# A two-layer hybrid trunk on one core: the last down projection with tokens on partitions, its norm by token blocks, and the token half moved outside the three products

## What is computed

```python
def rms_norm(x, w):
    y = x * lax.rsqrt(jnp.mean(x * x, axis=-1, keepdims=True) + NORM_EPS)
    return y * w

def swiglu(x, w_gate, w_up, w_down):
    return (jax.nn.silu(x @ w_gate) * (x @ w_up)) @ w_down
...
    for layer in range(DEPTH):          # 2
        nw = norm_w[layer]
        f = swiglu(rms_norm(h, nw[0]), ffn_w_gate[layer, 0], ffn_w_up[layer, 0], ffn_w_down[layer, 0])
        h = h + 0.5 * rms_norm(f, nw[1])
        ...                             # token mixer, residual
        f = swiglu(rms_norm(h, nw[4]), ffn_w_gate[layer, 1], ffn_w_up[layer, 1], ffn_w_down[layer, 1])
        h = h + 0.5 * rms_norm(f, nw[5])
    return h[:, N_META:]
```

## Time and profile before

| | |
|---|---|
| median of 3 runs | 2283.37 us (2280.93 to 2285.73) |
| the profiled execution | 2281.06 us |
| its span | 2279.3 us (first to last instruction), 1.8 us less |
| mean granted clock of TensorE | 0.979 of full speed |
| PE busy | 96% of the span, 16070 matmuls |
| DVE, ACT, POOL busy | 45%, 34%, 6% |

### The profile page before, as it was taken

One profiled execution on the slowest core, in us unless ns is written; L12 is line 12 of the kernel. 1 busy time (PEld: TensorE's weight loads), 2 busy tenths in 40 slices (PEclk: granted clock), 3 DMA queues, 4 the chain that ended last, 5 costly groups with the idle time before them and its releaser, 6 DMA issues.

```text
span 2279.3 us, 38433 instructions
## 1 busy us (share of the span) xinstructions
PE 2196.2 (96%) x16070; PEld 2065.8 (91%) x16070; DVE 1014.3 (45%) x1381; ACT 764.9 (34%) x1226; POOL 125.8 (6%) x119
## 2 busy tenths in 40 slices
PE   7999999998989899999999999999999999999997
PEld 6999999987889889999999999999998788888885
DVE  5444421654576365444216444421663446444313
ACT  3322222433433543222224322222452554222321
POOL 2000000000023010000000000000000020000001
PEclk9999999997899999999999999999999999999998
DMA  3332333321110013333321333332222122333430
GB/s 101 108 89 86 102 102 82 89 60 34 38 47 1 28 57 104 89 92 96 109 82 51 100 90 92 106 103 62 81 76 65 47 69 83 98 92 92 117 87 37
DMA packets 347340, 179.13 MB, mean 79 GB/s; under 512 B 15657, under 2 KB 345680, under 8 KB 347246
## 3 DMA queue, kind: packets, MB, share of 16 engines
q1 hardware_dynamic: 346032, 175.30, 26.6%
q0 software_dynamic: 880, 2.34, 0.5%
q10 hardware_dynamic: 334, 0.14, 0.0%
HBM read 175.64 MB, written 2.12 MB: 78 GB/s over the span
## 4 chain that ended last, share of the span: by engine, by line
PE 93%; DVE 4%; ACT 2%; issue 1%; DMA 0%; POOL 0%; ACTq 0%; DVEq 0%; POOLq 0%
PE psum L584 72%; PE psum L596 10%; PE psum L2175 1%; PE psum L1730 1%; PE psum L1744 1%; PE psum L2192 1%; DVE w_hl L513 1%; PE psum L1713 1%; PE psum L2639 0%; PE psum L1688 0%; PE psum L2655 0%; PE psum L2650 0%; DVE rinv L1289 0%; PE psum L650 0%; PE psum L674 0%
## 5 line engine op out<-in xcount | busy, mean ns | idle before, releaser
L584 PE MATMUL psum<-x_hl,w_hl 128*128 128x264 f32 (+1 forms) x9120 | 1247.2, 299 | 9.7 <-DVE x_hl L1225 4.1
L584 PEld LDWEIGHTS psum<-x_hl,w_hl 128*128 128x128 f32 x9120 | 1191.9, 190 | 62.0 <-issue 13.5
L513 DVE TENSOR_TENSOR w_hl<-stage,w_hl 128x1024 fp32r<-128x1024 f32 (+1 forms) x304 | 395.1, 1300 | 366.5 <-ACT w_hl L506 366.5
L584 PE MATMUL psum<-acts,w_hl 128*128 128x264 f32 (+1 forms) x2904 | 412.4, 304 | 0.0
L584 PEld LDWEIGHTS psum<-acts,w_hl 128*128 128x128 f32 x2904 | 388.3, 188 | 23.7
L506 ACT ACTIVATE w_hl<-stage 128x1024 fp32r<-128x1024 f32 (+1 forms) x304 | 338.2, 1113 | 187.9 <-PE psum L584 126.9
L1326 DVE TENSOR_TENSOR t_both<-psum,rinv 128x528 f32<-128x528 f32 (+1 forms) x88 | 61.9, 703 | 305.7 <-PE psum L584 305.7
L1113 ACT ACTIVATE acts<-t_both 128x528 f32 (+3 forms) x88 | 56.7, 644 | 403.6 <-DVE t_both L1329 403.6
L596 PE MATMUL psum<-x_hl,w_hl 128*128 128x264 f32 (+1 forms) x1344 | 174.2, 289 | 6.8 <-DVE w_hl L513 4.6
L596 PEld LDWEIGHTS psum<-x_hl,w_hl 128*128 128x128 f32 x1344 | 168.4, 191 | 9.9 <-DVE w_hl L513 5.0
L1320 DVE TENSOR_TENSOR t_both<-psum,rinv 128x528 f32<-128x528 f32 (+1 forms) x88 | 61.9, 703 | 183.5 <-PE psum L584 183.4
(11 more groups left out here) (327 smaller groups left out, 1310.5 us busy)
## 6 DMA issues: line engine op xcount, KB each, us to landing
stage<-ffn_w_gate SPq DMA_DIRECT2D x88, 512.0 KB, 3.8
stage<-ffn_w_up SPq DMA_DIRECT2D x88, 512.0 KB, 3.8
stage<-ffn_w_down SPq DMA_DIRECT2D x64, 704.0 KB, 4.4
stage<-odd_w_in SPq DMA_DIRECT2D x24, 512.0 KB, 3.8
stage<-even_w_in SPq DMA_DIRECT2D x18, 512.0 KB, 3.9
stage<-even_w_out SPq DMA_DIRECT2D x8, 512.0 KB, 4.0
stage<-odd_w_out SPq DMA_DIRECT2D x8, 512.0 KB, 3.9
rows_x<-x SPq DMA_DIRECT2D x1, 2048.0 KB, 10.5
```

The costliest lines, as they stand in the source:

```text
L513: dve.tensor_tensor(weights(core.w_hl[:, slot.ring, 1, :], *kind), weights(core.stage[:, slot.stage, :], *kind), weights(core.w_hl[:, slot ...
L584: op = pe.matmul(out, lhs, moving[:, moved, kt, t0:t0 + n], start=first and part + moved == 0, stop=last and part == 1)
```

## The change

It has two parts. In `products` the loop over token halves stands outside the loop over the three products: a half's three products follow each other into the same bank, then the other half's. The last down phase is of a new kind, `rows`. There the stationary operand is a block of 128 tokens of the activations and the moving one is 512 columns of a row of weights, so that results have tokens on partitions: 4 blocks x 2 halves of 512 features fill the 8 banks. The weights come as 22 slots of 128 input rows by 1024 (`load_slot`). The first four slots are used by blocks 0 and 1 first, with the 32 transposes of the residual between them, then by blocks 2 and 3; the last four slots are used block by block. Each block then gets its own norm: ACT squares and sums along the free dimension, DVE multiplies by the norm's weight (loaded as a row by POOL's queue), and one operation per half scales by the token's factor and adds the turned residual. SP stores halves of blocks. `token_factors`, the spreading, `vector_last`, `scale_results` and the transposes at the end are gone.

```diff
+ROW_HALF = D // 2
+ROW_BANKS = (5, 7, 4, 6)
...
             steps.append(("dense", Phase("gu", layer, 2 * FT, cols, n, ffn=ffn)))
+            if layer and ffn:
+                steps.append(("dense", Phase("rows", layer, FT, cols, n, ffn=ffn)))
+                return steps
...
+        self.h_rows = self.at("h_rows", [P, NBLK, D], self.x_at)
+        self.rows_out = self.at("rows_out", [P, NBLK, D], self.x_at + 4 * NBLK * D)
+        self.weight_row = self.t_both[:].rearrange("p a t -> p (a t)")[:, 0:D]
...
     for b in range(NBLK):
-        sp.wait_ge(core.out_left, b + 1)
-        sp.wait_ge(core.out_right, b + 1)
-        sp.dma_start(a["out"][0, b * P:(b + 1) * P, :], core.rows_out[:, b, :]).then_inc(core.out_stored, 16)
-    sp.wait_ge(core.out_stored, 16 * NBLK)
+        for half in range(2):
+            cols = slice(half * ROW_HALF, (half + 1) * ROW_HALF)
+            sp.wait_ge(core.rows_ready, 2 * b + half + 1)
+            sp.dma_start(a["out"][0, b * P:(b + 1) * P, cols], core.rows_out[:, b, cols]).then_inc(core.out_stored, 16)
+    sp.wait_ge(core.out_stored, 16 * 2 * NBLK)
...
+    if phase.kind == "rows":
+        rows = a["ffn_w_down"][phase.layer, phase.ffn][bass.ds(slot.local * P, P), :]
+        sp.dma_start(dst[:, 0:D], rows).then_inc(core.w_landed[slot.stage], 16)
+        return
...
 def products(core, pe, phase, slot, kt, w_tile, moving, first, last):
-    for part, moved in ((0, 0), (0, 1), (1, 0)):
-        lhs = core.w_hl[:, slot.ring, part, w_tile * P:(w_tile + 1) * P]
-        for b, (t0, n) in enumerate(halves(phase.cols)):
-            out = core.psum[:, 2 * slot.out_pair + b if slot.bank is None else slot.bank, 0:n]
+    for b, (t0, n) in enumerate(halves(phase.cols)):
+        out = core.psum[:, 2 * slot.out_pair + b if slot.bank is None else slot.bank, 0:n]
+        for part, moved in ((0, 0), (0, 1), (1, 0)):
+            lhs = core.w_hl[:, slot.ring, part, w_tile * P:(w_tile + 1) * P]
             op = pe.matmul(out, lhs, moving[:, moved, kt, t0:t0 + n], start=first and part + moved == 0,
                            stop=last and part == 1)
     return op
...
+def turned_residual(core, pe, first):
+    k = core
+    for j, bank in enumerate(ROW_BANKS):
+        b, half = first + j // 2, j % 2
+        for kt in range(DT // 2):
+            op = pe.transpose(k.psum[:, bank, kt * P:(kt + 1) * P],
+                              k.h[:, half * DT // 2 + kt, META + b * P:META + (b + 1) * P], k.ident[:])
+        op.then_inc(k.h_turned, 1)
+def row_products(core, pe, slot, kt, b):
+    k = core
+    for half in range(2):
+        for side, part in ((0, 0), (1, 0), (0, 1)):
+            op = pe.matmul(k.psum[:, 2 * b + half, :], k.acts[:, side, kt, META + b * P:META + (b + 1) * P],
+                           k.w_hl[:, slot.ring, part, half * ROW_HALF:(half + 1) * ROW_HALF],
+                           start=kt == 0 and side + part == 0, stop=kt == FT - 1 and part == 1)
+        if kt == FT - 1:
+            op.then_inc(k.rows_made, 1)
+    return op
+def tensor_rows(core, pe, phase):
+    k = core
+    slots = [Slot(phase, s // RING, s % RING) for s in range(FT)]
+    pe.wait_ge(k.scaled, phase.evac0 - 2)
+    for kt in range(RING):
+        pe.wait_ge(k.w_lo, slots[kt].count())
+        pe.wait_ge(k.act_lo, phase.a0 - FT + kt + 1)
+        for b in range(2):
+            row_products(k, pe, slots[kt], kt, b)
+        if kt == 0:
+            pe.wait_ge(k.scaled, phase.evac0)
+            turned_residual(k, pe, 0)
+        if kt == 2:
+            pe.wait_ge(k.h_left, 2)
+            pe.wait_ge(k.h_right, 2)
+            turned_residual(k, pe, 2)
+    pe.wait_ge(k.h_left, NBLK)
+    pe.wait_ge(k.h_right, NBLK)
+    for kt in range(RING):
+        for b in range(2, NBLK):
+            op = row_products(k, pe, slots[kt], kt, b)
+        op.then_inc(k.slot_used, 1)
+    pe.wait_ge(k.act_lo, phase.a0)
+    for kt in range(RING, FT - RING):
+        pe.wait_ge(k.w_lo, slots[kt].count())
+        for b in range(NBLK):
+            op = row_products(k, pe, slots[kt], kt, b)
+        op.then_inc(k.slot_used, 1)
+    for b in range(NBLK):
+        for kt in range(FT - RING, FT):
+            if b == 0:
+                pe.wait_ge(k.w_lo, slots[kt].count())
+            row_products(k, pe, slots[kt], kt, b)
...
-def token_factors(core, pe, norm):
...
+def scalar_rows(core, act, phase):
+    k = core
+    load_table(k, act, ACT.Sqrt)
+    split_ahead(k, act, split_hi, phase, 0, 0)
+    for b in range(NBLK):
+        act.wait_ge(k.h_turned, 2 * b + 1)
+        act.activation(k.h_rows[:, b, 0:ROW_HALF], k.psum[:, ROW_BANKS[2 * b % 4], :], ACT.Copy).then_inc(k.h_left, 1)
+    for s in range(1, FT - AHEAD):
+        split_ahead(k, act, split_hi, phase, s // RING, s % RING)
+    for b in range(NBLK):
+        act.wait_ge(k.rows_made, 2 * b + 1)
+        act.activation(k.sq_sum[:, 0:ROW_HALF], k.psum[:, 2 * b, :], ACT.Square,
+                       accum_out=k.by_token[:, 0, b:b + 1]).then_inc(k.rows_sq, 1)
+        act.wait_ge(k.rows_weighted, 2 * b + 1)
+        act.activation(k.rinv[:, 0:ROW_HALF], k.psum[:, 2 * b + 1, :], ACT.Square,
+                       accum_out=k.by_token[:, 1, b:b + 1]).then_inc(k.rows_sq, 1)
+        act.wait_ge(k.rows_sum, b + 1)
+        act.activation(k.by_token[:, 0, b:b + 1], k.by_token[:, 0, b:b + 1], ACT.Sqrt, bias=k.eps[:, 1:2],
+                       scale=4.0 / D).then_inc(k.rows_root, 1)
...
+def vector_rows(core, dve, phase):
+    k = core
+    split_ahead(k, dve, split_lo, phase, 0, 0)
+    for b in range(NBLK):
+        dve.wait_ge(k.h_turned, 2 * b + 2)
+        dve.tensor_copy(k.h_rows[:, b, ROW_HALF:D], k.psum[:, ROW_BANKS[2 * b % 4 + 1], :]).then_inc(k.h_right, 1)
+    for s in range(1, FT - AHEAD):
+        split_ahead(k, dve, split_lo, phase, s // RING, s % RING)
+    dve.wait_ge(k.weight_in, 16)
+    dve.wait_ge(k.h_left, NBLK)
+    dve.wait_ge(k.h_right, NBLK)
+    for b in range(NBLK):
+        for half in (1, 0):
+            cols = slice(half * ROW_HALF, (half + 1) * ROW_HALF)
+            if half:
+                dve.wait_ge(k.rows_made, 2 * b + 2)
+            else:
+                dve.wait_ge(k.rows_sq, 2 * b + 1)
+            dve.tensor_tensor(k.rows_out[:, b, cols], k.psum[:, 2 * b + half, :], k.weight_row[:, cols], ALU.mult)\
+               .then_inc(k.rows_weighted, 1)
+        dve.wait_ge(k.rows_sq, 2 * b + 2)
+        total = k.by_token[:, 0, b:b + 1]
+        dve.tensor_tensor(total, total, k.by_token[:, 1, b:b + 1], ALU.add).then_inc(k.rows_sum, 1)
+        dve.wait_ge(k.rows_root, b + 1)
+        dve.reciprocal(total, total).then_inc(k.rows_inverse, 1)
+        dve.wait_ge(k.rows_inverse, b + 1)
+        dve.wait_ge(k.rows_weighted, 2 * b + 2)
+        for half in range(2):
+            cols = slice(half * ROW_HALF, (half + 1) * ROW_HALF)
+            dve.scalar_tensor_tensor(k.rows_out[:, b, cols], k.rows_out[:, b, cols], total, k.h_rows[:, b, cols],
+                                     ALU.mult, ALU.add).then_inc(k.rows_ready, 1)
...
+        elif kind == "dense" and step.kind == "rows":
+            pool.wait_ge(k.act_lo, step.a0)
+            pool.dma_start(k.weight_row, a["norm_w"][1, 5:6, :].broadcast_to([P, D])).then_inc(k.weight_in, 16)
...
             odd_gpsimd(k, pool, step, a)
     pool.wait_ge(k.bias_stored, 16)
+    pool.wait_ge(k.weight_in, 16)
```

160 lines of the change are left out of this document (31 added, 129 removed).

## The result

| | before | after |
|---|---|---|
| median, runs taken side by side | 2282.26 us (4 runs, 2280.93 to 2285.73) | 2260.15 us (4 runs, 2258.26 to 2260.82) |
| ratio, 95% interval | | 0.9897 (0.9883 to 0.991) |
| the profiled execution | 2281.06 us | 2260.82 us |
| its span, mean granted clock | 2279.3 us, 0.979 | 2259.1 us, 0.980 |

A forecast was written before the change was run, and what follows sets the result against it. PE, busy for 96% of the span, was taken to bound the kernel, with 28.0 us behind its last product. 2281.06 - 17.7 + 1.4 = 2264.8, set at 2266 between the sums from profiled execution and median; range 2257 to 2275 us.

The forecast's parts named there:

- The end: Behind the last product: 28.0 us removed, replaced by one block's chain of 3.7 and a last store of 3.1, 6.8 us.
- The transposes: 32 of the residual, moved into two bursts of 16 among the row phase's first products: 3.5 us, 6.8 at the lower clock.
- The new phase: Last down phase: row products keep 232.6 ns and all waits are covered, tightest the last weight slot, 1.9 us to spare.
- The rows phase as a whole: Last down phase and what follows it: -28.0 + 3.5 + 6.8 = -17.7 us, bounds about -20 and -13.
- The token half outside: Phases on all tokens: no change for 8064 matmuls, +0.6 ns on each of 2376 in down phases, +1.4 us.
- the run of 111: A run of `part_products`, a half's three products in a row, at 121.7 ns like `products`: the sign for no change.
- its own test: Wrong if 1920 gate/up products shift over 1 us, row products leave 232.6 ns by over 2, or the row-phase clock falls.
- the order gains: Phases on all tokens: alternating banks or halves costs 0.5 to 1.8 ns, which the new order saves; 5 to 19 us, chance 0.13.
- the nearest row: Profile rows of `part_products`, which already makes a half's three products in a row, used to price the new loop order.
- the seam's slow rows: Down phases' seam: 147 matmuls at 122.7 ns, first 65 at 123.9; upper end +2.3 ns on each of 10,440, +24 us.

The follow-up runs named there:

- experiment 8: The changed kernel without the 32 transposes of the residual, their copies and waits, so the output lacks the residual: 2252.32 us, ratio 0.9866.
- experiment 2: The changed kernel with the old order inside `products` put back, so the rows phase and block norm alone: 2264.13 us, ratio 0.9922.
- experiment 1: The kernel before with the new loop order in `products` alone, its end unchanged: 2275.59 us, ratio 0.9971.
- experiment 3: The changed kernel with the two token halves reversed on odd input tiles: 2266.7 us, ratio 0.9926.
- experiment 4: The changed kernel with high weights on each half's high and low columns, then low weights on both halves: 2269.2 us, ratio 0.9942.
- experiment 5: The changed kernel with three variants by phase pair: old order moving one half only, new order likewise, old order into one bank: 2261.63 us, one run.
- experiment 6: The changed kernel with three variants by phase pair: new order into one bank, old and new order with high weights only: 2264.78 us, one run.
- experiment 7: The changed kernel with three other correct orders of the moving columns, one per pair of gate/up and down phases: 2263.8 us, one run.
- experiment 9: The changed kernel with the second half's moving columns starting at 256, 248 or 260 instead of 264, by block: 2264.77 us, one run.
- experiment 11: The changed kernel once more, unedited, run as a comparison beside the kernel before: 2257.7 us (2254.7 to 2263.0), ratio 0.9893.

## Why the prediction was right, and which step of it failed

*The end: right.* 28.0 us went, 6.15 came; 6.8 were costed. The chain took 3.6 (3.7 costed), and the store 2.55 instead of 3.1: the half block lands 0.5 us sooner, as the prediction had allowed for and not counted.

*The transposes: right.* 3.5 us by experiment 8, 3.5 costed, at clock 1.00 in both bursts. The Trainium skill, "TensorE: Matmul & The Clock Gate", Part 4 (PE-mode transpose), would have the full clock not engage for them. Here it stayed at 1.00 through them and behind them; the bursts are 1.9 us long and have products before and after, so this speaks for bursts like these alone.

*The new phase: right.* PE has no wait, not even before the last slot, to which 1.9 us of cover were given. Row products at 232.4 ns in the changed kernel's long run and 232.2 without transposes, 232.6 costed.

*The rows phase as a whole:* -17.7 costed; experiment 2 measured -17.8, by the profile it is -21.84 + 3.29 = -18.6. The last product ended at 2252.95 us instead of the forecast 2256: the order's gain came off it, less what the start and the first mixer lost.

*The token half outside: the step that failed.* The prediction took "no change for the 8064 (the run of 111 is of their kind) and +0.6 ns for the 2376", +1.4 us. Measured by the pace are -0.83 and -0.21 ns, -7.2 us, and by experiment 1's time -6.6: outside its own test ("if the run of 1920 in a gate/up phase lasts more than 1 us longer or less than before"; it was 1.59 less). The rival "the order gains", at a chance of 0.13 and with 5 to 19 us, is what happened, at its lower end and not by its mechanism: it blamed the alternation of banks or halves, and experiments 3 to 6 show that banks don't matter and that keeping to one half is slower than the new order. The error lies in what counted as the nearest row. `part_products` shares the order of the three products with the new loop, but it stays in one half from input tile to input tile, and the new loop changes half in every tile. By experiments 5, 7 and 9 the pace of a long run changes with just this sequence of moving columns. From the seam's slow rows (122.7, 123.9), equal in three phases, the prediction concluded that it is "a matter of where operands lie, not of chance". It isn't chance, but where they lie doesn't explain it alone: the next 65, with the same columns in the same turn, went at 122.0, and behind the new order the two parts changed places. The rows showed that one form of product can differ by 2 ns, and no sign for the new loop.

*The number:* from one profiled execution to the other, 1.46 us were lost before the first long run, the six long runs gained 5.3, layer 0's mixer lost 2.8 and what follows layer 1's first block gained 0.5 (both with their own products' gain in them), the row phase lost 3.3 and the end gained 21.8: -20.2 before rounding, and 2281.06 - 20.2 = 2260.8, as measured. The prediction had -17.7 + 1.4 = -16.3. Its one large miss is the order; the scatter of the start and the mixers hid part of it, and the range held the time since it took in part of the gaining order. That is luck in part: in experiment 11 the same kernel had a median of 2257.7, and two of its five runs, 2254.7 and 2255.03, lie below the range. The prediction also calls the profiled execution the second of three; it isn't one of them, which changes nothing in the sum.

## What to carry to other kernels

Ask of the end of a kernel that is bound by TensorE what stands behind its last matmul, and whether the last phase can be laid out so that its results finish block by block in the layout of the output: here that was worth 18 us for 32 transposes moved under full clock. Loop orders of matmuls that are equal in count are not equal in pace. Here it changed with the sequence of moving addresses and, in the seam, with what ran ahead, so take the price from a long run with the same sequence, or measure several orders in one kernel, one for each of its like phases. And where a kernel's time scatters by several us, compare the parts of two profiles between the same instructions before you believe a difference of the medians.

## What the runs showed of the hardware that was not expected

- The pace of long runs of 264-column matmuls on the full clock depends on where the moving columns are read from, matmul after matmul: 120.9 to 122.6 ns in gate/up and 121.1 to 123.5 in down phases for one count of columns (experiments 3 to 9). One bank or two, and one stationary tile or two, made no difference (experiments 5 and 6). The Trainium skill, "TensorE: Matmul & The Clock Gate", Back-to-back issue gap, gives N / 2.4 + 2.5 ns for the gap of a single matmul, an estimate of 112.5 for 264 columns; no sequence tried came nearer than 120.9.
- The same matmuls on the same columns, weights and banks went at 123.9 or 121.8 ns for 65 in a row, by the order of the products ahead of them (the two parts of the seam, before against after and experiment 1). Why isn't known.
- Moving the second half from column 264 to 256 made the down phase 2.1 ns slower per matmul.
- The same mixer, in executions of kernels that don't differ in it, took 464.6 to 472.2 us, with a mean clock of 0.94 to 0.92 around it. This scatter is larger than the effect of any single edit here but the rows phase.
- Storing half a block of 128 tokens (256 KB) lands in 2.1 us; a whole one took 2.6 to 3.4.
